# PEER layers: first expert rows fetched at down tile 12, and 16 more row dots placed between the ranking's steps

## What is computed

```python
def block(xb):                      # xb: 128 normed tokens
    q = (xb @ w_query).reshape(-1, 8, 2, 128)
    sc = jnp.einsum('thpc,hpkc->thpk', q, sub_keys)
    s1, i1 = lax.top_k(sc[:, :, 0], 16)
    s2, i2 = lax.top_k(sc[:, :, 1], 16)
    cand = (s1[..., :, None] + s2[..., None, :]).reshape(-1, 8, 256)
    top, ci = lax.top_k(cand, 16)
    ...
    idx = e1 * 128 + e2             # 8 heads x 16 experts of 16384
    g = jax.nn.softmax(top, axis=-1)
    hid = gelu(einsum('td,thkd->thk', xb, expert_down[idx]))
    return einsum('thk,thkd->td', g * hid, expert_up[idx])
```

## Time and profile before

| | us |
|---|---|
| median of 3 runs | 3308.85 (3308.65 to 3309.24) |
| the profiled execution, its own time | 3305.32 |
| its span, first to last instruction | 3303.6 |
| PE busy | 3242.8 (98%) |
| PE weight load busy | 2979.3 (90%) |
| VectorE busy | 1739.7 (53%) |
| ScalarE busy | 1392.5 (42%) |
| GpSimd busy | 1866.1 (56%) |
| TensorE's granted clock, mean over the span | 0.992 |

### The profile page before, as it was taken

The page is one execution under the profiler, slowest core; times in us unless marked ns, Lnnn a source line. Parts: engine busy times, 40 slices in busy tenths (PEclk is TensorE's granted clock), DMA queues, the critical chain, the costliest instruction groups (busy, mean ns, idle before and its releaser), DMA issues.

```text
span 3303.6 us, 48436 instructions
## 1 busy us (share of the span) xinstructions
PE 3242.8 (98%) x18888; PEld 2979.3 (90%) x18888; DVE 1739.7 (53%) x3840; ACT 1392.5 (42%) x2521; POOL 1866.1 (56%) x1079
## 2 busy tenths in 40 slices
PE   7998999999999999999999999999999999999999
PEld 6766899999999988888988878999999999888889
DVE  5254167996773444444432311789867634444443
ACT  4354233338884333333333332333488743333332
POOL 4323358986656355555354653689865564555552
PEclk9998999999999999999999999999999999999999
DMA  3211237888999688888532222489899987888883
GB/s 118 83 33 34 94 121 280 309 317 304 335 335 357 244 327 335 333 325 322 198 109 96 77 102 79 148 313 323 299 330 330 332 337 267 319 330 331 334 330 121
DMA packets 260227, 801.98 MB, mean 243 GB/s; under 512 B 23968, under 2 KB 73120, under 8 KB 259488
## 3 DMA queue, kind: packets, MB, share of 16 engines
q1 hardware_dynamic: 186272, 530.41, 44.5%
q0 software_dynamic: 73728, 268.47, 21.5%
HBM read 699.17 MB, written 99.61 MB: 242 GB/s over the span
## 4 chain that ended last, share of the span: by engine, by line
PE 82%; DVE 12%; issue 2%; POOL 1%; ACT 1%; DMA 1%; DVEq 0%; POOLq 0%; ACTq 0%
PE banks L254 21%; PE banks L256 21%; PE banks L255 21%; PE banks L1224 5%; PE banks L1260 4%; DVE arena L1304 2%; PE banks L269 1%; PE banks L270 1%; PE banks L271 1%; DVE arena L1379 1%; DVE gathered_rows L1304 1%; PE banks L1192 1%; PE banks L602 1%; DVE arena L1383 1%; DVE side L1321 1%
## 5 line engine op out<-in xcount | busy, mean ns | idle before, releaser
L221 POOL TENSOR_TENSOR weights_lo<-raw_ring,weights_hi 128x1024 fp32r<-128x1024 f32 x498 | 1247.9, 2507 | 1118.7 <-ACT weights_hi L215 1116.6
L254 PE MATMUL banks<-operand_hi,weights_hi 128*128 128x384 f32 (+1 forms) x4648 | 1604.0, 345 | 2.0 <-ACT arena L1100 1.2
L256 PE MATMUL banks<-operand_hi,weights_lo 128*128 128x384 f32 (+1 forms) x4648 | 1584.0, 341 | 0.0
L255 PE MATMUL banks<-operand_lo,weights_hi 128*128 128x384 f32 (+1 forms) x4648 | 1583.8, 341 | 0.0
L254 PEld LDWEIGHTS banks<-operand_hi,weights_hi 128*128 128x128 f32 x4648 | 872.9, 188 | 78.9 <-issue 54.3
L215 ACT CAST weights_hi<-raw_ring 128x1024 fp32r<-128x1024 f32 x624 | 653.4, 1047 | 641.2 <-PE banks L256 563.5
L255 PEld LDWEIGHTS banks<-operand_lo,weights_hi 128*128 128x128 f32 x4648 | 873.0, 188 | 21.4 <-issue 1.4
L256 PEld LDWEIGHTS banks<-operand_hi,weights_lo 128*128 128x128 f32 x4648 | 872.4, 188 | 21.7
L1462 DVE TENSOR_TENSOR residual<-residual,banks 128x384 f32<-128x384 f32 x256 | 141.9, 554 | 666.4 <-PE banks L256 666.4
L1100 ACT ACTIVATE arena<-banks 128x384 f32<-128x384 f32 x256 | 126.1, 493 | 540.3 <-PE banks L256 532.6
L1065 ACT CAST operand_hi<-arena 128x384 fp32r<-128x384 f32 x256 | 130.8, 514 | 267.7 <-DVE arena L1433 267.7
(11 more groups left out here) (210 smaller groups left out, 2902.3 us busy)
## 6 DMA issues: line engine op xcount, KB each, us to landing
raw_ring<-weight_tiles SPq DMA_DIRECT2D x624, 512.0 KB, 4.2
gate_scratch<-arena SPq DMA_DIRECT2D x24, 2048.0 KB, 14.4
arena<-gate_scratch SPq DMA_DIRECT2D x128, 384.0 KB, 7.6
hid_scratch<-arena SPq DMA_DIRECT2D x60, 768.0 KB, 7.3
arena<-hid_scratch SPq DMA_DIRECT2D x120, 384.0 KB, 5.9
arena<-up,side POOLq DMA_INDIRECT x146, 7.4
residual<-x_t SPq DMA_DIRECT2D x2, 1024.0 KB, 6.5
arena<-key_t SPq DMA_DIRECT2D x2, 1024.0 KB, 4.8
```

The lines of the kernel that those rows point to most:

```text
L221: eng.tensor_tensor(wl[:, b, :], raw[:, n % RING, :], wh[:, b, :].bitcast(F32), ALU.subtract).then_inc(done, 1)
L254: pe.matmul(out, w_hi, x_hi[:, c, :], start=start and c == 0, stop=False)
L255: pe.matmul(out, w_hi, x_lo[:, c, :], start=False, stop=False)
L256: last = pe.matmul(out, w_lo, x_hi[:, c, :], start=False, stop=stop and c == DC - 1)
```

## The change

The dots are split 76, 48 and 4 over the rankings, the units and the tail, where they were 60, 60 and 8. The first six fetches stand at down tiles 12 to 14 instead of 17 to 19. The 76 dots are expected at tiles 14 to 69 (56 tiles) instead of 60 at tiles 19 to 69 (51 tiles), and the fetches follow three tiles after the dot that frees their place. The number of dots, fetches and matmuls is unchanged. One wait is added on VectorE, ahead of a memset after the last dot, on a semaphore that VectorE itself raised.

```diff
--- before.py
+++ after.py
@@ -942,7 +942,7 @@
         UNIT_FROM = 73
         UNIT_TILE = [UNIT_FROM + u * 5 // 6 for u in range(UNITS)]
         TURN_TILE = UNIT_FROM - 3
-        ROUTE_DOTS, UNIT_DOTS, TAIL_DOTS = 60, 60, 8
+        ROUTE_DOTS, UNIT_DOTS, TAIL_DOTS = 76, 48, 4
         QUADS = G // 4
         DENSE = (0, 1, 7)
         QUAD_TILE = [13 + q * 32 // 10 for q in range(QUADS)]
@@ -961,7 +961,7 @@
         def dot_tile(k):
 
             if k < ROUTE_DOTS:
-                return 19 + k * 51 // ROUTE_DOTS
+                return 14 + k * 56 // ROUTE_DOTS
             k -= ROUTE_DOTS
             if k < UNIT_DOTS:
                 return UNIT_TILE[k * UNITS // UNIT_DOTS]
@@ -972,7 +972,7 @@
 
             return dot_tile(k) + (3 if k < ROUTE_DOTS else 1)
 
-        GATHER_DOWN_AT = [17 + k // 2 if k < DOWN_RING else after_dot(k - DOWN_RING) for k in range(P)]
+        GATHER_DOWN_AT = [12 + k // 2 if k < DOWN_RING else after_dot(k - DOWN_RING) for k in range(P)]
         UP_ORDER = [6] + [(P - DOWN_RING + i) % DOWN_RING for i in range(DOWN_RING)]
         GATHER_UP_AT = [PDOWN - 4] + [dot_tile(P - DOWN_RING + i) + 1 for i in range(DOWN_RING)]
         GATHER_UP_AT += [PDOWN + QUAD_TILE[(j - UP_RING) // 4] + 1 + (j - UP_RING) % 4 // 2 for j in range(UP_RING, P)]
@@ -1423,6 +1423,7 @@
                 dot_until(ROUTE_DOTS + UNIT_DOTS * (u + 1) // UNITS)
             dot_until(P)
             dve.wait_ge(s.g_scaled, was["g_scaled"] + UNITS)
+            dve.wait_ge(s.onehots, was["onehots"] + UNITS)
             dve.memset(side[:, 0:1088], 0.0).then_inc(s.z_cleared, 1)
 
             def gate_slice(g, j):
```

## The result

| | before | after |
|---|---|---|
| median of four runs, us | 3308.75 (3304.44 to 3309.24) | 3352.64 (3352.14 to 3353.04) |
| span of the profiled execution, us | 3303.6 | 3350.7 |
| mean granted clock | 0.992 | 0.987 |

The change costs 43.9 us, a ratio of 1.0133 with a 95% interval of 1.0120 to 1.0146. (The kernel before took from 3303 to 3320 us in thirteen executions on one chip, so where an experiment has one run, its whole time is good to some microseconds only and the stretches inside a layer tell more.) The forecast was 3339 us, with a range up to 3346: the direction was right, the size was not, and the time lies above the range.

The account below looks back on a forecast made before the run. PE was taken to set the pace inside a PEER layer, with one VectorE result 2.6 us late. 2 x (12.3 + 3.0) = 30.6 us on 3305.32 gives 3335.9; with the runs' median 3.5 us higher, 3339 us, range 3321 to 3346.

Parts of the forecast that it names:

- The start: VectorE's first dot: fetches from down tile 12 let it begin at about 508.1 instead of 527.29, 19.2 us earlier.
- The dots: VectorE's rankings: sixteen added dots cost their spacing of about 1.15 us each, +18.3 us per layer.
- The waits behind low halves: VectorE's ranking steps held by GpSimd's low halves: 18 waits, 27.7 us instead of 14.4, +13.3; bounds 0 and +34.
- hand rules: Fixed durations and precedence for carrying POOL's and VectorE's queues forward; the old order came out at 739.5 (trace 739.61).
- L1401 to the transposes: From VectorE's gates after the fourth ranking to PE's transposes: stays 3.65 us, so the transposes go at 755.6.
- The clock: PE behind the transposes' wait: a 6 us standstill lowers the granted clock, costing 3 us per layer; bounds 0 and 3.4.
- Units, tail and gathers: After the transposes: units lose 12 dots, the tail 4, and upward gathers go four tiles earlier, all at 0 us.
- POOL's load of 102%: GpSimd's work per ranking of 17 tiles: 72.5 us of 70.8 with 76 dots, where it was 97%.
- Rival 3: Not slower: VectorE's waits stay 14.4 us if POOL keeps under 100% of a ranking's time; 3307 us, chance 10%.
- rival 1: PE's stalls come as forecast but the granted clock holds: 3333.5 us, chance 20%.
- Rival 2: VectorE and POOL collisions fall out of step, only half the extra ones come, +5 per layer: 3319 us, chance 14%.
- Rival 4: VectorE's first dot waits longer because early fetches share the DMA; 3 us more would give 3345; chance 6%.

Follow-up runs that it names:

- experiment 7: The changed kernel with GpSimd's low halves of down tiles 14 to 71 cut to 896 of 1024 columns: 3328.99 us.
- experiment 9: The changed kernel with sixty idle matmuls on PE ahead of the transposes' wait, to keep PE busy: 3346.07 us.
- the eight traces: Traces of the kernel before, the changed kernel and six variants: early start alone, dots alone, casts as tensor_tensor, 68 dots, 72 dots, idle matmuls on PE.

## Why the prediction was wrong, point by point

**The start, -19.2 us at the first dot.** The first dot begins 61.4 us behind tile 0 where it began 82.5, so -21.1. The expert numbers came as forecast, but the first row took 5.3 us to its dot and not 7.4. Timeline, GpSimd and VectorE:

```profile
502.40 1.08 POOL L1152 DMA_INDIRECT pair<-down,side  x1 [0.93 <-DVE side L1396]
...
507.74 1.22 DVE L1304 CUSTOM_DVE_ANT_0 pair<-pair,banks 128x1024 f32<-128x1024 f32 x1 [2.53 <-DMA pair<-down,side]
```

**The dots, +18.3 us.** Measured 91.1 - 72.9 = 18.3.

**The waits behind low halves, 27.7 - 14.4 = +13.3 us: this is the step that failed.** Measured as above, 36.7 - 13.4 = +23.3. The 14.4 for the old order was right within 1 us, and low halves are the cause, as forecast: with short ones all of it is gone. But the extra did not come where the forecast put it. It had 18 waits, 27.7 us, of steps that run into a low half; 11 such steps came, 15.9 us, hardly more than the 9 and 14.1 of the old order. The hand rules had the door closed for the 2.40 us of a low half, and the time of the fetch ahead of it they took to be free. There 8 steps were held, 21.6 us, a term that stood at nothing: seven of them at 2.7 to 3.1 us in the last two rankings of layer 0. In the old order no step fell into that time, so rules without it could reproduce it. My bound, +34, held; my choice inside it rested on rules that fitted the old order alone, and that it was off by only 10 us is in part luck: one error was 12 us too much, the other 22 too little. The terms now sum to 18.3 - 21.1 + 23.3 = 20.5 us against 12.3.

**A coupling that the rules had, but too late.** With VectorE late, GpSimd waits for a dot before it may refill that row's place, and the low halves queue behind:

```profile
652.74 0.95 POOL L1152 DMA_INDIRECT arena<-down,side  x1 [4.16 <-DVE side L1304]
653.99 1.57 POOL L1152 DMA_INDIRECT pair<-down,side  x1 [0.30 <-issue]
655.58 2.35 POOL L221 TENSOR_TENSOR weights_lo<-raw_ring,weights_hi 128x1024 fp32r<-128x1024 f32 x1
```

PE's stalls were forecast at tiles 34, 50, 52, 53, 62, 67 and 70, 9.0 us; they came at 34, 50, 52, 53, 62, 69 and 70, 12.5 us in layer 0. That they cost nothing of their own held: experiment 7 removed them and left the wait at the turn.

**L1401 to the transposes, 3.65 us.** Held: the transposes' wait ends by the same chain, and tile 71 starts 5.7 us behind L1401 where it started 4.7; the 1.0 us more is the clock.

**The clock, 3 us per turn.** The dip came, at waits of 10.4 and 11.4 us instead of 6. By experiment 9 it cost 1.8 and 2.4 us, 4.1 for both turns and not 6.

**Units, tail and gathers, 0.** Held: behind tile 73 each tile takes what it took before, to 0.03 us.

**POOL's load of 102%.** Held as the cause of PE's stalls: at seven eighths of a low half they went, with a third of the holding. It is not what starts the holding: 64 dots load POOL to 96% by the same sum (63.2 + 4.8 of 70.8 us), and VectorE is held 33 to 35 us. Rival 3 (not slower), which was to be decided at 100%, is refuted by both; so is rival 1 (the clock holds). Rival 2's point, that a meeting depends on tenths of a microsecond, is what the row with 68 dots shows, only the sum went the other way. (Its own 3319 us lies outside the range that was to take in most of it.) Rival 4's cause, rows that come late, did not happen with 76 dots: VectorE waits 12.0 us for rows, once a layer at the first dot (4.9 us together) and once at the last ones. With 68 it did, nine times up to L1401 in layer 0, 11.1 us.

**The rule of the Trainium skill.** Page "SBUF — State Buffer", section "Who interferes with whom", has it that a tensor_tensor with both inputs in SBUF contends with GpSimd's reads, and infers that descriptor generation stays free of it. The runs ask for both sides to be told apart. A fetch does wait for a running tensor_tensor: in the kernel before, each of the twelve beside an L1379 or L1381 ended 0.82 to 0.83 us behind that step, after up to 2.83 us. But a fetch holds no VectorE step (0 of 69), and what stands behind it does.

**Best version.** The early start with 60 dots: 3304.13 us, within 0.8 us of the kernels with short low halves. In this stretch PE is busy without a break, so more from the dots is not to be had.

## What to carry over

Work moved onto an engine costs its own duration and the meetings it shifts. Where two engines hold each other up, first measure the unheld time of the waiting one (here by cutting the other's work short); the difference is a budget that can be followed from kernel to kernel. Rules that reproduce the old order prove nothing about a case that the old order does not contain: sort the held steps by what the other engine did when they began, and see whether the new order adds a kind. And gathering DMA issues has a price: it leaves compute instructions without a break between them, and a step may wait for two of them.

## What the runs showed of the hardware

- A VectorE step with both sides in SBUF (cast, tensor_scalar, scalar_tensor_tensor, tensor_tensor alike) is shut out from about 0.62 us before the record of a GpSimd compute instruction that stands ready behind a fetch: 3.03 us for 0.22 (637.32), 73 of 83 such steps. Where two low halves follow each other at once it may have to wait for both (5.45 us, and 7.53 us for L1379) or be let in between (3.19 us at 562.27 of the grouped fetches).
- A memset of one column, 0.11 us, between fetch and low half does not let it in.
- A fetch that begins beside an L1379 or L1381 ends 0.82 to 0.83 us behind it, twelve of twelve in the kernel before.
- Not all steps are shut out. The dots, which have one operand in PSUM, take 1.21 to 1.23 us in all 2048 cases of the eight traces, 90 of them begun up to 0.62 us ahead of a ready low half; the reductions L1383 take 2.28 to 2.29 us in all of theirs, and a cast from PSUM took 0.28 us at 754.14 with 68 dots, with a low half 0.37 us behind its begin.
- The first ranking is not stable to 3 us between programs that are alike up to there: L1396 comes 55.5 us behind layer 0's tile 0 in the changed kernel and the one with the early start alone, 58.1 with 68 and 72 dots, and with 64 dots 55.5 in layer 0 and 58.1 in layer 1, by whether one L1379, begun 39.25 us behind tile 0 in all of them, takes 2.29 or 4.5 us. Where it was late, the first fetch waited 4.3 us for GpSimd's numbers instead of 0.9, and PE lost 2.2 to 2.3 us at tiles 15 to 17. What tips it was not tried.
